# Far keys by quarters of the head dimension, a shared query tile, gate stores on SP's queue, and near scores in plain fp32, in the attention stage of a one-core decoder layer

## The reference

```python
h = x @ w_in + b_in                      # q, k, v of 3 x 8 heads x 128, z_b, u, v_a, z_a, g_a, g_b
q, k = rope(q, pos), rope(k, pos)
# three dilation groups (window, dilation) = (128,1), (512,4), (2048,16):
# query t reads keys t, t-d, ..., t-window; the sample tokens read their caches and the new keys
s = einsum('bthe,btjhe->bthj', q, keys_gathered) * dh ** -0.5
o_b = merge_dilation_groups([softmax(s) @ v for each group])
y_a, v_rows = gmlp_branch(u, v_a, z_a, ...)
merged = sigmoid(g_a) * (y_a @ w_o_a) + sigmoid(g_b) * ((o_b * silu(z_b)) @ w_o_b)
x = layer_norm(alpha * x + merged @ w_out)
```

## Time and profile before

| | |
|---|---|
| median of 3 runs | 2698.89 us (2698.2 to 2701.54) |
| profiled execution, its time | 2696.65 us |
| its span | 2695.0 us |
| TensorE busy | 2326.3 us, 86% |
| VectorE busy | 1623.4 us, 60% |
| ScalarE busy | 928.7 us, 34% |
| GpSimd busy | 300.4 us, 11% |
| data moved by DMA | 384.04 MB |
| mean granted TensorE clock | 0.937 |

### The profile page before, as it was taken

One profiled execution on the slowest core, in us unless ns is written; L12 is line 12 of the kernel. 1 busy time (PEld: TensorE's weight loads), 2 busy tenths in 40 slices (PEclk: granted clock), 3 DMA queues, 4 the chain that ended last, 5 costly groups with the idle time before them and its releaser, 6 DMA issues.

```text
span 2695.0 us, 44546 instructions
## 1 busy us (share of the span) xinstructions
PE 2326.3 (86%) x17744; PEld 2271.8 (84%) x17744; DVE 1623.4 (60%) x2118; ACT 928.7 (34%) x1334; POOL 300.4 (11%) x508
## 2 busy tenths in 40 slices
PE   5999999999999999995858586776858598999994
PEld 5999999999999999995757585666858588999994
DVE  7677787867777777774545444354545456553336
ACT  4444444444444444442313131222313142332222
POOL 0100000000000000003221221211221210000003
PEclk8999999999999999997889797888989799999997
DMA  4434343433333333447554555645554545344332
GB/s 142 130 118 122 117 123 117 121 118 114 114 116 115 117 113 119 135 122 261 161 200 135 204 154 171 222 146 192 173 192 132 183 128 184 111 128 151 103 104 90
DMA packets 405692, 384.04 MB, mean 143 GB/s; under 512 B 16033, under 2 KB 360113, under 8 KB 404737
## 3 DMA queue, kind: packets, MB, share of 16 engines
q1 hardware_dynamic: 358560, 196.84, 25.4%
q0 software_dynamic: 46944, 184.44, 20.1%
HBM read 334.84 MB, written 46.37 MB: 141 GB/s over the span
## 4 chain that ended last, share of the span: by engine, by line
PE 68%; DVE 12%; DMA 12%; POOL 3%; issue 2%; ACT 2%; SPq 0%; ACTq 0%; DVEq 0%; POOLq 0%
PE acc L671 42%; PE acc L725 19%; DMA qb<-q_scratch 6%; DVE far L1411 2%; DVE qb L1410 2%; DMA raw<-in_w_in 2%; DMA cache<-in_cache_v 2%; PE scp L780 1%; PE scp L807 1%; DVE wl L1225 1%; ACT wh L930 1%; PE turn L745 1%; POOL qu L537 1%; DVE sc L1438 1%; PE turn L680 1%
## 5 line engine op out<-in xcount | busy, mean ns | idle before, releaser
L671 PE MATMUL acc<-xh,wph 128*128 128x288 f32 x2912 | 868.6, 298 | 37.1 <-DVE wpl L1225 28.6
L671 PE MATMUL acc<-xl,wph 128*128 128x288 f32 x2912 | 860.8, 296 | 0.0
L671 PE MATMUL acc<-xh,wpl 128*128 128x288 f32 x2912 | 857.8, 295 | 0.0
L671 PEld LDWEIGHTS acc<-xh,wph 128*128 128x128 f32 x2912 | 547.5, 188 | 39.0 <-issue 22.4
L671 PEld LDWEIGHTS acc<-xh,wpl 128*128 128x128 f32 x2912 | 550.0, 189 | 0.0
L671 PEld LDWEIGHTS acc<-xl,wph 128*128 128x128 f32 x2912 | 548.5, 188 | 0.0
L1225 DVE TENSOR_TENSOR wl<-raw,wh 128x512 fp32r<-128x512 f32 x256 | 176.7, 691 | 397.1 <-ACT wh L930 397.0
L930 ACT ACTIVATE wh<-raw 128x512 fp32r<-128x512 f32 x256 | 160.9, 629 | 665.5 <-PE acc L725 609.0
L725 PE MATMUL acc<-xh,wh 128*128 128x288 f32 x1024 | 241.1, 318 | 5.9 <-DVE wl L1225 3.0
L725 PE MATMUL acc<-xl,wh 128*128 128x288 f32 x1024 | 225.9, 303 | 0.0
L725 PE MATMUL acc<-xh,wl 128*128 128x288 f32 x1024 | 225.2, 302 | 0.0
(11 more groups left out here) (222 smaller groups left out, 3941.1 us busy)
## 6 DMA issues: line engine op xcount, KB each, us to landing
raw<-in_w_in SPq DMA_DIRECT2D x128, 256.0 KB, 3.4
qb<-q_scratch POOLq DMA_DIRECT2D x64, 512.0 KB, 7.7
cache<-in_cache_v POOLq DMA_DIRECT2D x64, 448.0 KB, 7.2
w_a<-in_w_in SPq DMA_DIRECT2D x52, 512.0 KB, 3.8
w_c<-in_w_in SPq DMA_DIRECT2D x52, 512.0 KB, 3.8
w_b<-in_w_in SPq DMA_DIRECT2D x52, 512.0 KB, 3.8
w_d<-in_w_in SPq DMA_DIRECT2D x52, 512.0 KB, 3.9
ones<-in_ones_k POOLq DMA_DIRECT2D x64, 256.0 KB, 6.1
```

What stands on the lines that cost most here:

```text
L671: done = pe.matmul(bank, w[ring][:, k, :], a[x][:, k, :], start=(j in (0, 1, 3, 5) and k == 0 and t == 0), stop=(k == HK - 1 and t == 2), ...
```

## The change

- The far keys are laid out by quarters of the head dimension: a partition holds 32 of the 128 dimensions of 4 x 32 key positions. The query rows that a partition needs are then the same quarter of the 64 rows, 8 KB for all eight sequences; they are loaded once a head (`load_queries`), and kept. The product goes to a tile of its own (`prod`), and the sum over 32 dimensions leaves four partial sums in four partition groups; a matmul with a matrix of stacked 32 x 32 identities (`sums`) adds them and turns them at once. The far columns go. The `units` follow the same layout.
- The scratch in DRAM holds the rows by quarters; it is written by two DMAs.
- The near scores are 8 plain fp32 matmuls on `near` and `qz`; `kth`, `ktl`, `qzh` and `qzl` go. The early scores come at slot 2.
- The gate stores go from POOL's queue to SP's, each after the load of a block's fourth quarter.
- y is made in place of z (`zt`), not in `yt`; so `load_head`, which overwrites it, waits for the store of y.
- The order in POOL's queue is another one.

```diff
-SLOT_KT, SLOT_EARLY, SLOT_FAR, SLOT_PTS = 0, 3, 22, 27
+SLOT_EARLY, SLOT_FAR, SLOT_PTS = 2, 22, 27
...
-    qs_d = dram("q_scratch", HEADS, 2, SAMP, P)
+    qs_d = dram("q_scratch", HEADS, 2, 4, SAMP, 32)
...
+            def store_gate(n):
+                sp.wait_ge(acc_read, n + 1)
+                sp.dma_start(gate_d[n], gstage[:]).then_inc(g_stored, 16)
...
                     load(QUARTERS * (f - 1) + u,
                          quarter_of(w_in, QB * (u % 4), COL_GA + (gate_block(f, u // 4)) * P))
+                    n = gate_block(f, u // 4) - 1
+                    if u % 4 == 3 and n >= 0:
+                        store_gate(n)
...
-                pool.dma_start(qs_d[ds(f, 1)].rearrange("o g s d -> s (o g) d"), qn[SAMP:P]).then_inc(q_stored, 16)
+                for g in range(2):
+                    pool.dma_start(qs_d[ds(f, 1), g].rearrange("o c s d -> s (o c) d"),
+                                   qn[SAMP:P, g, :].rearrange("p (c d) -> p c d", d=32)).then_inc(q_stored, 16)
...
+            def load_queries(h):
+
+                if h > 0:
+                    pool.wait_ge(ones_sum, 8 * h)
+                for c in range(4):
+                    pool.dma_start(qb[32 * c:32 * c + 32].rearrange("p b t d -> p (b t) d"),
+                                   qs_d[h:h + 1, 0, c].broadcast_to([32, SAMP, 32])).then_inc(q_in, 16)
+
             def load_ones(h, b):
...
-                pool.dma_start(ones[:, b % 2, :, :], ones_k[h, b]).then_inc(ones_in[b % 2], 16)
-                pool.dma_start(qb[:, b % 2, :, :], qs_d[h:h + 1, 0, DEC_T * b:DEC_T * b + DEC_T, :]
-                               .broadcast_to([P, DEC_T, P])).then_inc(ones_in[b % 2], 16)
+                pool.dma_start(ones[:, b % 2, :], ones_k[h, b]).then_inc(ones_in[b % 2], 16)
...
+                load_ones(h, 2)
+                load_ones(h, 3)
                 if h > 0:
                     store_y(h - 1)
-                if f < HEADS:
-                    load_head(f, 1 - par)
                 for b in range(4):
                     load_values(h, b)
-                load_ones(h, 2)
-                load_ones(h, 3)
+                if f < HEADS:
+                    if h > 0:
+                        pool.wait_ge(y_stored, 16 * h)
+                    load_head(f, 1 - par)
+                load_ones(h, 4)
+                load_ones(h, 5)
                 if f < HEADS:
                     pool.wait_ge(scored, signal_no(f, "early"))
                     load_near(f)
-                load_ones(h, 4)
+                load_ones(h, 6)
                 load_units(h, 1)
+                load_ones(h, 7)
                 if f == HEADS:
                     pool.wait_ge(y_stored, 16 * (HEADS - 1))
                     pool.dma_start(yb_raw[:], yb_d[0:HEADS - 1].rearrange("h p c -> p h c")).then_inc(yb_in, 16)
-                load_ones(h, 5)
-                store_gate(0)
-                load_ones(h, 6)
-                load_ones(h, 7)
-                store_gate(1)
-                if f < HEADS:
+                else:
                     load_ones(f, 0)
                     load_ones(f, 1)
+                    load_queries(f)
                     load_units(f, 0)
-                store_gate(2)
                 for b in range(4, 8):
                     load_values(h, b)
-                store_gate(3)
...
+                    for j in range(4):
+                        pe.matmul(scp[0:SAMP, SEQ + 32 * j:SEQ + 32 * j + 32], far_1[:, j, :], sums[:, 0:32],
+                                  start=True, stop=True)
+                    pe.matmul(scp[0:SAMP, SEQ + P:SEQ + 2 * P], far_2[:], sums[:], start=True, stop=True
+                              ).then_inc(scored, 1)
...
-                    q1 = qb[:, b % 2, :, :].rearrange("p (u c) d -> p u (c d)", u=2)
-                    keys = ones[:, b % 2, :, :].rearrange("p c d -> p (c d)").rearrange("p (o x) -> p o x", o=1)
-                    links.then(v.tensor_tensor(q1, q1, keys.broadcast_to([P, 2, 4 * P]), ALU.mult))
-                    v.tensor_reduce(far_1[:, b, :], qb[:, b % 2, :, :], mybir.AxisListType.X, ALU.add
-                                    ).then_inc(ones_sum, 1)
+                    keys = ones[:, b % 2, :].rearrange("p (j o x) -> p j o x", j=4, o=1).broadcast_to([P, 4, 2, P])
+                    rows = qb[:, b, :, :].rearrange("p t d -> p (t d)").rearrange("p (o u x) -> p o u x", o=1, u=2)
+                    links.then(v.tensor_tensor(prod[:], keys, rows.broadcast_to([P, 4, 2, P]), ALU.mult))
+                    v.tensor_reduce(far_1[:, :, DEC_T * b:DEC_T * b + DEC_T],
+                                    prod[:].rearrange("p j u (c d) -> p j (u c) d", d=32),
+                                    mybir.AxisListType.X, ALU.add).then_inc(ones_sum, 1)
```

More of the change, by code:

```diff
@@ L206, in build @@
         qkv = put("qkv", 2, HEAD_ROW)
-        yt, qzh, qzl = put("yt", TOK), put("qzh", TOK, dt=F32R), put("qzl", TOK, dt=F32R)
+        qz = put("qz", TOK)
+        far_1, far_2, otmp = put("far_1", 4, SAMP), put("far_2", SAMP), put("otmp", SAMP)
+        psn, smask, sums = put("psn", GROUPS, SAMP), put("smask", KEYS + NEW), put("sums", P)
         GQ = GROUPS * TOK
@@ L219, in build @@
         vl = sb("vl", [P, 4, 7, P], place_v, F32R)
-        place_n = place_v + 28 * P * 4
         near = put("near", DEC_B * P)
[L222 to L225, removed]
+        qb = put("qb", DEC_B, DEC_T, 32)
+        qu, units = put("qu", 4, DEC_T, 32), put("units", 4, DEC_T, 32)
+        ones, prod = put("ones", 2, 4 * P), put("prod", 4, 2, P)
+        place_s = place_v + (28 + 56) * P * 4
         vh = [put("vh0", 7, P, dt=F32R), put("vh1", 7, P, dt=F32R)]
         sc = sb("sc", [P, 6 * P], place_s)
-        kth = sb("kth", [P, DEC_B * P], place_s, F32R)
         pt = sb("pt", [P, 6 * P], place_s + CACHED * 4)
@@ L412, in branch_block @@
                     load(q0 + 2 * n + v, quarter_of(w_o, QB * v, n * P))
+                if q0 == Q_B and n == 1:
+                    store_gate(2 * KB - 1)
             def load_gate(n, g):
@@ L533, in load_units @@
                     pool.wait_ge(units_sum, 2 * h + half)
[L534 to L537, removed]
+                pool.dma_start(units[:].rearrange("p b t d -> p (b t d)"), units_k[h, half]).then_inc(units_in, 16)
+                for c in range(4):
+                    pool.dma_start(qu[32 * c:32 * c + 32].rearrange("p b t d -> p (b t) d"),
+                                   qs_d[h:h + 1, 1, c, 32 * half:32 * half + 32, :].broadcast_to([32, 32, 32])
                                    ).then_inc(units_in, 16)
@@ L556, in _ @@
             pool.wait_ge(pre_split, 1)
-            for dst, src in ((mask, c_mask), (smask, c_smask)):
+            for dst, src in ((mask, c_mask), (smask, c_smask), (sums, c_sum)):
                 pool.dma_start(dst[:], src).then_inc(consts, 16)
@@ L756, in early_scores @@
                     bank_free("early")
-                    pe.wait_ge(q_spread, 2 * f)
-                    pe.wait_ge(near_split, f)
+                    pe.wait_ge(q_spread, f)
+                    pe.wait_ge(near_in, 16 * f)
                     for b in range(DEC_B):
[L760 to L764, removed]
+                        pe.matmul(scp[0:SAMP, 0:P], qz[:, SAMP * b:SAMP * b + SAMP], near[:, b * P:(b + 1) * P],
+                                  start=(b == 0), stop=(b == DEC_B - 1), skip_group_check=True)
                     for g in range(GROUPS):
@@ L1414, in far_units @@
                 def far_units(h, half):
                     dve.wait_ge(units_in, 80 * (2 * h + half + 1))
+                    if half == 0 and h > 0:
+                        dve.wait_ge(scored, signal_no(h, "far"))
                     links.then(v.tensor_tensor(qu[:], qu[:], units[:], ALU.mult))
-                    v.tensor_reduce(far_2[:, 4 * half:4 * half + 4, :].rearrange("p b u -> p (b u)"), qu[:],
+                    v.tensor_reduce(far_2[:, 32 * half:32 * half + 32], qu[:].rearrange("p b t d -> p (b t) d"),
@@ L1458, in frame @@
                             continue
-                        if s == SLOT_KT:
-                            dve.wait_ge(near_round, f)
-                            low(ktl[:], near[:], kth[:]).then_inc(near_split, 1)
                         for b in range(DEC_B):
```

86 lines of the change are left out of this document (34 added, 52 removed).

## The result

The changed kernel takes 2506.07 us (median of 4 runs, 2504.2 to 2510.55) against 2699.29 us: a ratio of 0.9286, 95% interval 0.927 to 0.9302. The prediction was 2505 us. The profiled execution is the slowest of the four, 2510.55 us with a span of 2508.9 us; against the 2695.0 us of before it is 186 us shorter, where the medians differ by 193 us.

What follows compares the result with a forecast made beforehand. Bound: TensorE idle in the attention frames behind VectorE's late `qb` transfers. Gains of 145 us (frames 2 to 7), 29 (frame 8) and 20 (frame 1), total 194, took 2696.65 to 2503, plus 2.2 for the median: 2505 us; range 2455 to 2580.

Steps and rivals of the forecast that it cites:

- What bounds it: Attention frames: TensorE idle some 33 of 121 us, waiting for VectorE behind late `qb` transfers; 32.8 us lost per frame.
- The broadcast: Query rows per head: 1 MB loaded once, 3.1 MB less per frame; multiply and reduce 1.22 us each, at most twice that.
- The third rival: Queries and units broadcast in 128-byte packets, 16384 per frame; some 10 us per frame lost, 2585 us; chance 0.06.
- Order: POOL's queue: `ones` 2 and 3 land early; `ones` 4 lands at t0 + 18.8, TensorE waits 6.3 us before slot 8.
- the bound of 23.5: Latest landing of `ones` 4 after t0: its issue at 9.5 plus the 13.95 us that `qb` needed; loss 12.2 us.
- The clock term: TensorE's clock falls again after the wait before slot 8, costing 2.6 us per frame.
- Gate stores on SP: Weight load behind `store_gate` goes out at t0 + 2.2, lands at t0 + 15, hidden by 0.9 us; other boundaries cost nothing.
- Near and far scores: TensorE's fp32 score matmuls: near +0.4 us, far +0.7 us, together +1.1 us per frame.
- Frame 1: First attention frame: 37 us of gain, 17 given back because the burst starves the weights, 20 us kept.
- The wait comes back at tile 4: Rival: `ones` 4 lands at t0 + 23.5, loss 12.2 us per frame; 2550 us, or 2566 with weights; chance 0.20.
- Slower by SP's queue: Rival: TensorE waits over 8 us at each of four boundaries for weights behind `store_gate`; with 10 us, 2765 us; chance 0.04.
- The scratch: Each head's 64 KB store, in 128-byte runs, would take longer, but lies in the projection off the path: no term.

Runs made afterwards that it cites:

- the 16 us: Kernel before with only the new POOL order and gate stores on SP: 2517.9 us, 0.9347; the changed kernel's ratio lies 16 us of 2700 below it.
- the run with both edits: Changed kernel with `ones` 4 issued ahead of the wait for y's store and the head, and each gate store one load later: 2450.2 us, 0.9067.

## Why the prediction was right, point by point

**What bounds it.** Right: 176 of the profiled 186 us lie in frames 2 to 8, most of it as idle time of TensorE. One statement was wrong: frame 8 took 115.5 us, not 121, and frames 2 to 7 took 121.9.

**The broadcast.** Each multiply and reduce takes 1.22 us in the new strides too, the lower bound that I took. That fewer bytes were no term of their own in the sum is borne out by the run that put them back; what waits for the bytes (ones 4 and `qb` 4 together) is in the 16 us. The third rival, 128-byte packets, did not happen: 36992 packets of POOL's queue for 149.90 MB are 4.05 KB each.

**Order.** Right: tiles 2, 3 and 5 stopped waiting, and ones 4 became the next late one. The term for it was mis-sized: 6.3 us forecast, 11.4 us in the frame shown, 9.3 us on average of the six. The issue came earlier than forecast (t0 + 5.8 to 7.4 against 7.5 to 9.5), the landing later: t0 + 21.1 on average and 22.4 in the frame shown, against 18.8, inside the bound of 23.5. The other part of the miss is TensorE, which reaches the turn at t0 + 15.1 on average (14.3 in the frame shown) against 15.9. What failed in the landing is the count of the bytes. Windows over the burst, the last two columns the DMA share and GB/s:

```profile
1643.00:1645.00 2.00, 2.00 (x19) 1.83 (x18) 1.90 (x3) 0.63 (x1) 1.50 (x3) 1.00 0.78 226
1645.00:1650.00 5.00, 5.00 (x38) 4.45 (x37) 2.82 (x6) 0.00 (x0) 3.04 (x6) 1.00 1.01 393
1650.00:1655.00 5.00, 4.44 (x34) 4.21 (x32) 0.00 (x0) 0.00 (x0) 0.00 (x0) 1.00 1.05 383
1655.00:1658.00 3.00, 0.00 (x0) 0.00 (x0) 0.00 (x0) 0.00 (x0) 0.00 (x0) 1.00 1.04 380
1658.00:1661.00 3.00, 0.00 (x0) 0.00 (x0) 1.92 (x7) 0.63 (x1) 0.00 (x0) 0.51 1.03 372
1661.00:1663.00 2.00, 0.00 (x0) 0.00 (x0) 0.46 (x2) 1.03 (x2) 0.00 (x0) 0.50 0.95 264
...
1666.00:1671.00 5.00, 5.00 (x18) 3.97 (x19) 3.65 (x6) 0.87 (x2) 1.93 (x4) 0.50 0.28 78
```

From t0 to the landing of ones 4 (1640.14 to 1662.56 us) the queues moved (packets, MB, share):

```profile
q0 software_dynamic: 1397, 6.19, 75.5%
q1 hardware_dynamic: 2095, 1.27, 19.0%
```

That is 7.5 MB (6.6 to 7.5 in the six frames), and I had counted 6.2: 5.4 on POOL's queue up to ones 4 itself, and 0.8 on SP's. So 0.75 MB of what stands behind ones 4 in its own queue (ones 5 and near) went ahead of its end, and SP's queue moved 0.5 MB more than I took. At the burst's 384 GB/s the difference is 3.2 us of the 3.6 by which it landed late. The clock term was right: 1.00 to 1658, then the low level, and 5 us of work at 0.50 after the wait.

**Gate stores on SP.** The mechanism was right and the cover was there (0.9 us forecast, 1.5 us in the frame shown, 2.3 us on average). The load took 12.9 to 14.3 us in five frames and 16.1 us in the one shown, where it left at t0 + 2.0 and ScalarE had it at t0 + 18.1; I took 12.72 us from the one row. The run with the stores one load later shows that it cost nothing, the run with both edits that it was the next in line. The benefit is another matter. I priced the move at "0 to 2 us, taken as nothing", yet the sum had most of it in other terms: y's store at t0 + 0.3 instead of t0 + 2.4, and ones 2 and 3 in SBUF before the frame. The runs say that the stores' old places would have cost 48 us. In a sum that a reader can check it should have stood as a term of its own.

**Near and far scores.** The eight near matmuls take 1.96 us on TensorE, 24 took 1.6: +0.4 as taken. The far ones take 0.90 us from first start to last end where two transposes took 0.38: +0.5, taken at +0.7.

**What made up for the longer wait.** TensorE's waits per frame in frames 2 to 7 sum to 34.2 us before and 12.4 after (205.4 and 74.2 in six frames), 21.9 us less; the forecast has 27.3 - 4.9 = 22.4. In it the turns gain 3.2 us a frame, and they lost 1.2 (51.0 to 58.0 us in six frames), an error of 4.4; against it stand the 2.4 us of the cached values and the 0.8 us before L792 of then, which I had costed at nothing, and 0.6 us more before the first scores. The rest of a frame, in which TensorE works, went from 87.7 to 84.9 us: 2.8 us, where the forecast has 5.5 - 2.6 - 1.1 = 1.8 for the clock and the added matmuls. So the mechanism was right, but that 24.7 per frame lies within 1 us of 24.2 is partly luck: two errors of about 4 us with opposite signs.

**Frame 1.** 13 instead of 20 us. The give-back that I guessed at 17 was 24. Three kinds of wait show there, two of them for weights (`raw`, 16.1 us of ScalarE's waits, 10.15 the longest, and 6.1 us on TensorE for `wl`), one before the first scores (6.3 us), behind VectorE's wait for ones. No run took this frame apart, so their shares stay open, as does the -3.4 us after y_done of frame 8; the traces of the other runs have 487.2 to 489.1 us there, so that most of it is probably what executions differ by. For the profiled pair the forecast of 194 us is 8 too many; the medians, 193 apart, are what it meets.

**The rivals.** "The wait comes back at tile 4" came nearly true for the landing (t0 + 22.4 of 23.5 in the worst frame, 21.1 on average), but not for the time, because of the terms above. "Slower by SP's queue" did not happen: no wait of L736 in frames 2 to 7. As to the Trainium skill (DMA: Bandwidth & Descriptors, Queues, rings and completion order), by which an engine takes turns between queues packet by packet, the trace agrees, if what the profile counts as packets are these: from 1647 to 1661 us the two queues had nearly as many each:

```profile
q0 software_dynamic: 1118, 4.80, 89.4%
q1 hardware_dynamic: 1131, 0.58, 14.1%
```

What the prediction read as sharing badly is this sharing, seen in bytes: a packet of SP's queue is 0.5 KB here and one of POOL's 4.3 KB, so SP's queue got 11% of the bytes. In frame 8, which loads no head, the weight quarter took 9.4 us instead of 12.9 to 16.1.

**The scratch.** Each of its two 32 KB stores lands 1.9 us after its issue, where the one of 64 KB took 2.0. Whether the 128-byte runs are slower is not shown by that; they cost no time that can be seen.

## What to carry to other kernels

- When a transfer is late, add up everything that moves until it lands, on every queue, and not only what stands in front of it in its own; here that is 7.5 MB against 6.2. What stands far enough behind it does not count: 1 MB more there changed nothing.
- Two late transfers that end within some 2 us of each other hide each other: removing one gave 1 us, the other 25, both 56. Look for what is second before you judge an edit by its run alone.
- A store that must wait for another engine should not stand in a queue ahead of loads that the next stage needs. Which queue it is on made no difference (2502 and 2506 us); its place in the order was worth 48 us.
- Read more than one frame before you compare two runs: the frame shown is the worst of six, and landings differ by up to 3 us between frames of one trace.

## What the runs showed of the hardware

- 3.1 MB per head of DMA traffic more, 1 MB of it in the burst behind `ones` 4, cannot be seen in the time (2511.8 against 2506.1 us) nor in the landing of `ones` 4 (t0 + 19.7 to 22.2 against 19.6 to 22.4). With y's store 2.1 us or more later (t0 + 2.4) and the head 3 us or more later (t0 + 6.6 to 7.4), `ones` 4 lands at t0 + 22.5 to 23.4.
- In a burst that holds the DMA share above 1.0 for 16 us, landing order was close to one common end: ones 4, issued at 1646.4, and near, issued 1.8 us later, landed within 3 us of each other (16.1 and 16.7 us after issue).
- In that burst SP's and POOL's queues moved 1131 and 1118 packets, and 0.58 and 4.80 MB: the queue with the short packets gets as many turns and few bytes.
